# Both ways from the mixers to the experts, token tile by token tile

## The reference, cut to what matters

```python
def hier_moe(x, w_group, b_group, w_expert, b_expert, w1, w3, w2):       # second stage, 32 experts
    g_logits = xf @ w_group + b_group;  g_sel = argmax(g_logits);  g_w = softmax(g_logits)[g_sel]
    e_logits = (xf @ w_expert + b_expert)[the 8 of the group g_sel]
    e_top, e_loc = top_k(e_logits, 2);  gate = g_w * softmax(e_top)
    out[token] += gate * ((silu(x @ w1[e]) * (x @ w3[e])) @ w2[e])      # for its two experts

def expert_choice_ffn(h, w_router, w_gate, w_up, w_down):                # first stage, 16 experts
    aff = softmax(h @ w_router);  gate, idx = top_k(aff.T, 32)           # each expert takes 32 tokens
    y = (silu(h[idx] @ w_gate) * (h[idx] @ w_up)) @ w_down * gate        # added back at idx

def first_block(...):
    x = x + m2 * (mix @ w_out);  h = rmsnorm(x, norm2_g) * (1 + m4) + m3
    x = x + m5 * expert_choice_ffn(h, ...);  return rmsnorm(x, final_norm_g)
def second_block(...):
    h = h + g1 * ((ga * y_a + gb * y_b) @ w_out);  u2 = rmsnorm(h, norm2_g) * (1 + sc2) + sh2
    h = h + g2 * hier_moe(u2, ...);  return rmsnorm(h, final_g)
```

## Time and profile before

| what | value |
|---|---|
| median of three runs | 2306.96 us (2306.05 to 2314.09) |
| the profiled execution | 2308.12 us, its span 2306.3 us |
| TensorE matmul | 1898.4 us busy, 82% of the span |
| VectorE, ScalarE, GpSimd | 509.6, 319.9 and 97.7 us busy |
| moved by DMA | 728.67 MB, mean 316 GB/s |
| mean granted TensorE clock | 0.848 of full speed |

### The profile page before, as it was taken

How to read it: one execution, slowest core, us unless ns; L and a number is a source line. 1 busy time by engine, 2 the same in 40 slices (tenths; PEclk the granted TensorE clock), 3 DMA queues, 4 the chain that set the end, 5 groups by cost and what they waited for, 6 DMA issues and landing times.

```text
span 2306.3 us, 30312 instructions
## 1 busy us (share of the span) xinstructions
PE 1898.4 (82%) x12166; PEld 1059.0 (46%) x12166; DVE 509.6 (22%) x1047; ACT 319.9 (14%) x592; POOL 97.7 (4%) x125
## 2 busy tenths in 40 slices
PE   6999998867676767676766767799999599999997
PEld 3676776742222222222222222688788344444443
DVE  3224563330000000000000000342521312222222
ACT  3123331010000000000000000211520100000001
POOL 1012211000000000000000000000200000000000
PEclk9999999867667677777677676799999799999999
DMA  8214556079999999999999999244344699999997
GB/s 337 90 38 165 206 200 229 34 288 423 422 422 422 422 422 422 422 422 422 423 422 422 422 422 422 100 135 144 122 144 148 262 418 421 422 422 422 422 422 295
DMA packets 102752, 728.67 MB, mean 316 GB/s; under 512 B 11440, under 2 KB 12048, under 8 KB 16144
## 3 DMA queue, kind: packets, MB, share of 16 engines
q1 hardware_dynamic: 99504, 717.04, 76.4%
q10 hardware_dynamic: 3168, 10.49, 1.3%
HBM read 726.39 MB, written 1.10 MB: 315 GB/s over the span
## 4 chain that ended last, share of the span: by engine, by line
PE 66%; DMA 24%; DVE 4%; issue 3%; ACT 2%; POOL 0%; DVEq 0%; SPq 0%; ACTq 0%; POOLq 0%
DMA ring<-in_w_down 18%; PE psum L499 9%; PE psum L712 9%; PE psum L851 7%; PE psum L487 5%; PE psum L746 4%; DMA ring<-in_w_mod 4%; PE psum L1147 3%; PE psum L526 3%; PE psum L723 2%; PE psum L693 2%; DMA ring<-in_moe_w 2%; PE psum L1136 2%; PE psum L1081 2%; PE psum L979 2%
## 5 line engine op out<-in xcount | busy, mean ns | idle before, releaser
L499 PE MATMUL psum<-ring,main 128*32 128x512 f32 x2048 | 277.7, 692 | 85.0 <-ACT main L573 35.0
L518 PE MATMUL psum<-ring,main 128*32 128x512 f32 x1024 | 176.1, 808 | 84.8 <-DMA ring<-in_w_down 72.4
L712 PE MATMUL psum<-ring,main 128*64 128x512 f32 x1024 | 226.4, 594 | 2.3 <-DMA ring<-in_moe_w 1.3
L499 PEld LDWEIGHTS psum<-ring,main 128*32 128x32 f32 x2048 | 65.2, 123 | 281.0 <-issue 184.5
L851 PE MATMUL psum<-main,ring 128*128 128x256 f32 x768 | 169.2, 380 | 0.0
L851 PEld LDWEIGHTS psum<-main,ring 128*128 128x128 f32 x768 | 146.0, 190 | 21.7 <-issue 0.5
L712 PEld LDWEIGHTS psum<-ring,main 128*64 128x64 f32 x1024 | 72.5, 137 | 151.1 <-issue 149.8
L487 PE MATMUL psum<-main 128*128 128x32 f32 x512 | 112.5, 402 | 33.8 <-DVE main L551 33.8
L487 PEld LDWEIGHTS psum<-main 128*128 128x128 f32 x512 | 110.4, 332 | 57.5 <-DVE main L551 57.5
L518 PEld LDWEIGHTS psum<-ring,main 128*32 128x32 f32 x1024 | 30.7, 134 | 211.0 <-DMA ring<-in_w_down 145.1
L558 DVE TENSOR_TENSOR main<-main,psum 128x512 f32<-128x512 f32 x16 | 11.0, 688 | 525.1 <-ACT main L576 525.1
(11 more groups left out here) (422 smaller groups left out, 2056.5 us busy)
## 6 DMA issues: line engine op xcount, KB each, us to landing
ring<-in_moe_w SPq DMA_DIRECT2D x192, 1024.0 KB, 17.0
ring<-in_w_gate SPq DMA_DIRECT2D x128, 1024.0 KB, 25.9
ring<-in_w_up SPq DMA_DIRECT2D x128, 1024.0 KB, 25.9
ring<-in_w_down SPq DMA_DIRECT2D x128, 1024.0 KB, 20.4
ring<-in_w_mod SPq DMA_DIRECT2D x48, 1024.0 KB, 6.9
ring<-in_w_in SPq DMA_DIRECT2D x36, 1024.0 KB, 4.9
ring<-in_w_out SPq DMA_DIRECT2D x8, 1024.0 KB, 5.7
ring<-in_w_rnn_out SPq DMA_DIRECT2D x8, 640.0 KB, 3.9
```

Source lines behind the costliest of these rows:

```text
L499: last = mm(psum[32 * j:32 * j + 32, b, :], xg1[:, k, :], slot(n % SLOTS)[:, 512 * j:512 * j + 512], start=k == 0, stop=k == KT - 1)
L518: last = mm(psum[q:q + 32, BANK_Y, :], hidT[:, P * (f % 4) + 32 * (f // 4):P * (f % 4) + 32 * (f // 4) + 32], w[:, r, 512 * g:512 * g + 51 ...
L712: last = nc.tensor.matmul(psum[CAP2 * u:CAP2 * u + CAP2, b, :], xg2[:, 4 * h + k, CAP2 * u:CAP2 * u + CAP2], w[u][:, k, :], start=h == 0 a ...
```

## The change

- **First way.** The gain row is made before the late adds. The norm works on halves of a tile and signals each. The router holds the router weights as stationary operand, padded to 32 columns, four feature chunks side by side in the four column groups; the four partial sums are copied out and added by one matmul with a constant (`sum_experts`). It runs tile by tile, as do maximum, exponent, reciprocal and product. The rounds of the choice read PSUM in the first round instead of a copy; the product of the gates comes after the signal for positions; `slot` counts from 1, so the subtraction of 1 goes.
- **First expert stage.** One-hots of both tiles come first and have their own signal; gated ones follow (`m_gated`). ScalarE's two copies signal separately (`m_spread_sb`). A Silu of one column is called ahead of the loop.
- **Second way.** The projection goes tile by tile; norm, turn and router of tile 0 stand between the column blocks of tile 1. The norm takes two operations per half. The router holds 64 columns of weights, two chunks side by side. Three small operations of the choice are merged into others, the index and one-hots of a tile follow its choice at once, the gates of tile 1, the gated columns, the count and the flag come after the first one-hots. Only the three banks that the first gather uses are waited for ahead of it.
- **Loads.** SP loads slots 4 to 11 first, at `mixers_done`, then 0 to 3. In block 2 it loads six slots once the mixers' values are ready (`mix2_ready`), the other six behind the projection.

```diff
+    pe.wait_ge(m_gated, e + 1)
+    pe.wait_ge(m_spread_sb, e + 1)
...
-        pos = pg_tm[:, 0, t, bass.ds(e, 1)]
-        V.tensor_scalar(onehot[:, t, 0:CAP1], K("slot")[:, 0:CAP1], pos, None, ALU.is_equal)
+        last = V.tensor_scalar(onehot[:, t, 0:CAP1], K("slot")[:, 0:CAP1], pg_tm[:, 0, t, bass.ds(e, 1)], None, ALU.is_equal)
+    last.then_inc(m_onehot, 1)
+    for t in range(NT):
         last = V.tensor_scalar(gated[:, t, :].rearrange("p (g s) -> p g s", g=4),
                                K("slot")[:, 0:CAP1].unsqueeze(1).to_broadcast([P, 4, CAP1]),
-                               pos, pg_tm[:, 1, t, bass.ds(e, 1)], ALU.is_equal, ALU.mult)
-    last.then_inc(m_onehot, 1)
+                               pg_tm[:, 0, t, bass.ds(e, 1)], pg_tm[:, 1, t, bass.ds(e, 1)], ALU.is_equal, ALU.mult)
+    last.then_inc(m_gated, 1)
...
+    act.activation(xg1.rearrange("p k s -> p (k s)"), psum[:, BANK_X, 0:KT * CAP1], ACT.Copy).then_inc(m_xg, 1)
     act.wait_ge(m_spread, 2 * e + 1)
-    act.activation(xg1.rearrange("p k s -> p (k s)"), psum[:, BANK_X, 0:KT * CAP1], ACT.Copy)
-    act.activation(spread, psum[:, BANK_P, 0:S], ACT.Copy).then_inc(m_xg, 1)
+    act.activation(spread, psum[:, BANK_P, 0:S], ACT.Copy).then_inc(m_spread_sb, 1)
...
+    def project_out2(t, c):
+        key = ("wo2", t, c // 2)
         pe.wait_ge(*arrived(("w_out_2", c)))
         w = chunk(("w_out_2", c)).rearrange("p (k n) -> p k n", k=KT)
-        o = banks.new(("wo2", c))
-        pe.wait_ge(*banks.free(("wo2", c)))
...
+        if c % 2 == 0:
+            banks.new(key)
+            pe.wait_ge(*banks.free(key))
+        o = banks.tile(key)[:, 256 * (c % 2):256 * (c % 2) + 256]
         for k in range(KT):
-            last = mm(o[:, NE * t:NE * t + NE], u2T[:, k, P * t:P * t + P], w_rt2[:, k, :], start=k == 0, stop=k == KT - 1)
-    last.then_inc(banks.when_full("rt2"), 1)
+            last = mm(o, mixT2[:, k, P * t:P * t + P], w[:, k, :], start=k == 0, stop=k == KT - 1)
+        if c % 2:
+            last.then_inc(banks.when_full(key), 1)
+        last_user[("w_out_2", c)] = key
+
+    def turn_u2(t):
+        for g in range(2):
+            o = banks.new(("u2T", t, g))
+            pe.wait_ge(*banks.free(("u2T", t, g)))
+            pe.wait_ge(u2_ready, 2 * t + g + 1)
+            for c in range(4):
+                last = flip(o[:, P * c:P * c + P], u2[:, t, P * (4 * g + c):P * (4 * g + c) + P])
+            last.then_inc(banks.when_full(("u2T", t, g)), 1)
+
+    def route2(t):
+        o = banks.new(("rt2_part", t))
+        pe.wait_ge(*banks.free(("rt2_part", t)))
+        pe.wait_ge(wrt_loaded, 32)
+        for k2 in range(4):
+            if k2 % 2 == 0:
+                pe.wait_ge(*banks.read_out(("u2T", t, k2 // 2)))
+            for j in range(2):
+                last = mm(o[64 * j:64 * j + 64, 0:P], w_rt2[:, 2 * k2 + j, :], u2T[:, 2 * k2 + j, P * t:P * t + P], start=k2 == 0, stop=k2 == 3)
+        last.then_inc(banks.when_full(("rt2_part", t)), 1)
+
+    def route2_sum(t):
+        o = banks.new(("rt2", t))
+        pe.wait_ge(*banks.free(("rt2", t)))
+        pe.wait_ge(*banks.read_out(("rt2_part", t)))
+        mm(o[:, 0:NG2 + E2], rt2_part[:, t, :], K2("sum_experts_2"), start=True, stop=True).then_inc(banks.when_full(("rt2", t)), 1)
+
+    for c in range(4):
+        project_out2(0, c)
+    project_out2(1, 0)
+    project_out2(1, 1)
+    turn_u2(0)
+    project_out2(1, 2)
+    route2(0)
+    project_out2(1, 3)
+    route2_sum(0)
+    turn_u2(1)
+    route2(1)
+    route2_sum(1)
 
     o = banks.new("pos2")
     pe.wait_ge(*banks.free("pos2"))
     pe.wait_ge(masks_ready, 1)
     mm(o[:, 0:E2], K("tri_f"), masks[:, 0, :], start=True, stop=True)
     mm(o[:, E2:2 * E2], ones, masks[:, 0, :], start=True, stop=False)
-    mm(o[:, E2:2 * E2], K("tri_f"), masks[:, 1, :], start=False, stop=True)
-    mm(o[:, 2 * E2:3 * E2], ones, masks[:, 0, :], start=True, stop=False)
...
     for free in (n_gathered, n_gates, n_turned, n_spread):
         pe.sem_inc(free, 1)
-    gather2(pe, 0)
+    pe.wait_ge(masks_ready, 2)
+    mm(o[:, E2:2 * E2], K("tri_f"), masks[:, 1, :], start=False, stop=True).then_inc(banks.when_full("pos2"), 1)
+    o = banks.new("count2")
+    pe.wait_ge(*banks.free("count2"))
+    mm(o[:, 0:E2], ones, masks[:, 0, :], start=True, stop=False)
+    mm(o[:, 0:E2], ones, masks[:, 1, :], start=False, stop=True).then_inc(banks.when_full("count2"), 1)
+    used_first = (BANK_XG, BANK_XG + 1, BANK_P2)
+    assert banks.order["count2"] % 8 not in used_first, banks.order["count2"] % 8
+    for b in used_first:
+        pe.wait_ge(*banks.last(b))
+    gather2(pe, 0, first=True)
...
+    def route(t):
+        o = banks.new(("rt_part", t))
+        pe.wait_ge(*banks.free(("rt_part", t)))
+        pe.wait_ge(wrt_loaded, 16)
+        for k2 in range(2):
+            pe.wait_ge(*banks.read_out(("h2T", t, k2)))
+            for j in range(4):
+                last = mm(o[32 * j:32 * j + 32, 0:P], w_rt[:, 4 * k2 + j, :], h2T[:, 4 * k2 + j, P * t:P * t + P], start=k2 == 0, stop=k2 == 1)
+        last.then_inc(banks.when_full(("rt_part", t)), 1)
+        o = banks.new(("rt", t))
+        pe.wait_ge(*banks.free(("rt", t)))
+        pe.wait_ge(*banks.read_out(("rt_part", t)))
+        mm(o[:, 0:E1], rt_part[:, t, :], K("sum_experts"), start=True, stop=True).then_inc(banks.when_full(("rt", t)), 1)
...
-    for n in range(SLOTS):
-        if n == FRONT:
-            sp.wait_ge(mixers_done, 1)
-        if n < FRONT:
-            sp.wait_ge(*banks.full(last_user[holder1[n]]))
+    sp.wait_ge(mixers_done, 1)
+    for n in range(FRONT, SLOTS):
+        moe1_load(sp, 0, n)
+    for n in range(FRONT):
+        sp.wait_ge(*banks.full(last_user[holder1[n]]))
         moe1_load(sp, 0, n)
...
-    for n in range(12):
-        if n == FRONT:
-            sp.wait_ge(mixers_done, 2)
-        if n < FRONT:
-            sp.wait_ge(*banks.full(last_user[holder2[n]]))
+    sp.wait_ge(mix2_ready, KT // 2)
+    for n in (4, 5, 8, 9, 10, 11):
+        moe2_load(sp, 0, n)
+    for n in (0, 1, 2, 3, 6, 7):
+        sp.wait_ge(*banks.full(last_user[holder2[n]] if n < FRONT else ("wo2", 1, 1)))
...
+    act.activation(rstat[:, 31:32], half, ACT.Silu).then_inc(act_step, 1)
...
     for half_ in range(2):
         add_mix(1, half_, EARLY)
+    dve.wait_ge(rows_loaded[0], 64)
+    dve.wait_ge(gain_loaded, 16)
+    V.scalar_tensor_tensor(rows[:, 1, :], rows[:, 1, :], 1.0, gain, ALU.add, ALU.mult).then_inc(dve_step, 1)
+    dve.wait_ge(dve_step, dve_steps())
     for t in range(NT):
...
+    o = banks.tile("affT")[0:E1, 0:S]
+    for r in range(CAP1 // 8):
+        left = work if r else o
+        V.max(top8[0:E1, :], left).then_inc(dve_step, 1)
+        dve.wait_ge(dve_step, dve_steps())
+        V.match_replace(work, top8[0:E1, :], left, -1.0).then_inc(dve_step, 1)
+        dve.wait_ge(dve_step, dve_steps())
+    V.tensor_scalar(tmp, work, -1.0, None, ALU.is_equal).then_inc(dve_step, 1)
+    dve.wait_ge(dve_step, dve_steps())
+    V.tensor_tensor_scan(pos, a0, tmp, 0.0, ALU.mult, ALU.add).then_inc(dve_step, 1)
+    dve.wait_ge(dve_step, dve_steps())
+    V.tensor_tensor(pos, pos, tmp, ALU.mult).then_inc(dve_step, 1)
+    dve.wait_ge(dve_step, dve_steps())
+    dve.sem_inc(choice_ready, 1)
+    V.tensor_tensor(gat, o, tmp, ALU.mult).then_inc(banks.when_read("affT"), 1)
...
+    for half_ in range(2):
+        add_mix2(0, half_)
     dve.sem_inc(x3_ready, 1)
-    dve.sem_inc(mixers_done, 1)
     dve.wait_ge(rows_loaded[1], 48)
     dve.wait_ge(gain_loaded, 48)
     V.scalar_tensor_tensor(rows2[:, 1, :], rows2[:, 1, :], 1.0, acc2[:, 0, :], ALU.add, ALU.mult).then_inc(dve_step, 1)
     dve.wait_ge(dve_step, dve_steps())
-    dve.wait_ge(rstd_ready, 7)
-    for t in range(NT):
...
+    norm2_2(0)
+    for half_ in range(2):
+        add_mix2(1, half_)
+    dve.sem_inc(x3_ready, 1)
+    norm2_2(1)
...
+    gates_of(0)
     dve.wait_ge(*banks.full("pos2"))
-    o = banks.tile("pos2")
-    V.tensor_tensor(pos2, o[:, 0:2 * E2].rearrange("p (t e) -> p t e", t=NT), masks, ALU.mult).then_inc(dve_step, 1)
...
+    V.tensor_tensor(pos2, banks.tile("pos2")[:, 0:2 * E2].rearrange("p (t e) -> p t e", t=NT), masks, ALU.mult).then_inc(banks.when_read("pos2"), 1)
+    dve.wait_ge(*banks.read_out("pos2"))
+    dve.wait_ge(n_gathered, 1)
+    for t in range(NT):
+        for u in range(2):
+            last = V.tensor_scalar(onehot2[:, t, CAP2 * u:CAP2 * u + CAP2], K("slot"), pos2[:, t, u:u + 1], None, ALU.is_equal)
+    last.then_inc(n_onehot, 1)
+    gates_of(1)
+    for t in range(NT):
+        for u in range(2):
+            last = V.tensor_scalar(gated2[:, t, CAP2 * u:CAP2 * u + CAP2], K("slot"), pos2[:, t, u:u + 1], gates2[:, t, u:u + 1],
+                                   ALU.is_equal, ALU.mult)
+    last.then_inc(n_gated_first, 1)
```

(51 more changed lines are left out.)

253 lines of the change are left out of this document (105 added, 148 removed).

## The result

The changed kernel takes **2295.6 us** (median of 11 runs, 2284.1 to 2302.9), the kernel before 2308.6 beside it (11 runs, 2301.1 to 2314.1): ratio **0.9938, 95% interval 0.992 to 0.9956**. The profiled execution took 2295.71 us with a span of 2293.9, so 12.4 us less span than before.

The account below looks back on a forecast made before the run. Both expert stages were taken as bound by their weight stream (the second partly by TensorE), counted from their first up matmuls. 2308.12 - 7.7 (first way) - 16.3 (second way) = 2284.1 profiled, so median 2283; range 2276 to 2294.

Parts of the forecast that it names:

- The rule of the sum: Both expert stages: a microsecond earlier at either first up matmul is one less at the end, if twelve loads are in.
- I take 7.9: landing 463.7: First way: gain row lands 7.9 us after issue beside eight loads, at 463.7; last late add ends at 470.8.
- The late bound: First way: rows land only with all eight loads, at 478; late adds end at 485, up matmul 6.5 us later.
- Rows starve: Rival, first way: ScalarE's queue gets little while SP's is full, landing 478, time 2297 us; chance 0.06.
- One of the two ways is given back: Rival: product waits to about 470, or tables stay and second start finds 1.2 GHz; 2288 to 2293 us; chance 0.12.
- A + 27.95: First way: up matmul starts 27.9 to 28.0 us after the last late add ends, at 498.8, 7.7 us earlier.
- The gain product's new place: First way: product before the late adds, its 1.23 us falling into VectorE's idle 4.49 us before 461.26.
- that lower case: First way, rows in time: tile 1's adds wait only for TensorE, late adds end at 467.9, up 10.6 us earlier.
- The table load: First expert loop: the 1.28 us load before ScalarE's 0.39 us copy should go, a Silu being called before the loop.
- Second way: Second projection to second up matmul: up at 1816.4 instead of 1832.69, 16.3 us earlier, through router, choice and masks to gather.
- Clock: TensorE's rise from 1.2 GHz may shift: first gather up to 3 us shorter, second up to 2.5 shorter or 1 longer.
- clock rises sooner: Rival: rows land in time and the clock rises sooner in the first way, 2277 to 2280 us; chance 0.18.

Follow-up runs that it names:

- small_packets: Changed kernel with the first eight loads of the first experts each issued as two DMAs of 4 KB per partition: 2285.6 us, one run.
- rows_alone: Changed kernel, but SP issues its first loads of slots 4 to 11 only once norm rows and gain have landed: 2283.5 us, ratio 0.9869; again 2282.9, 0.9881.
- no_silu: Changed kernel without the Silu called ahead of the first expert loop: 2302.3 us, one run.
- rows_first_plus: rows_alone with the gain product back between the tiles' late adds and the gathered rows' copy released by the gather alone: 2284.7 us, ratio 0.9904.
- late_loads2: Changed kernel, but the second way's six early loads wait for the end of the projection: 2296.7 us, ratio 0.994.

## Why the prediction was wrong, point by point

- **The rule of the sum** holds: pairs keep their 29.0 and 29.8 us, and the span after the second up matmul is 473.6 us before (2306.3 - 1832.69) and 473.7 after (2293.9 - 1820.22).
- **"I take 7.9: landing 463.7"** is the step that failed. The gain landed at 473.0 (456.79 + 16.2). The end of the late adds, A, was to be at R + 17.05 (470.8 - 453.75) and came at R + 25.59 (480.31 - 454.72): **8.5 us**.
- **The late bound has the right kind of mechanism and a number that is near by luck.** With all eight loads first (landing 478, time 2297) it is the rival "Rows starve", and the result lies 1.4 us from its price. But the gain landed at 473.0, when 4.4 of the 8.4 MB had passed, and the first way lost 2.2 us and not the 6.5 of that bound; what it lacks cancels part of that: the kernel before stood at 2308.6 and not 2307, and the start and the stage between took 1.5 us more. The rival "One of the two ways is given back" (0.12) names the very wait, to about 470, and prices it at 2288 to 2293; the wait ended 3 us later. I gave "Rows starve" 0.06 and excluded it with the Trainium skill's rule ("DMA: Bandwidth & Descriptors", Queues, rings and completion order) that an engine alternates between queues packet by packet. The trace agrees that the queues alternate: 638 packets against 602. It doesn't agree with the packet of 9 to 17 descriptors that the Trainium skill gives there, if a record of the trace is a descriptor: the turns here are single records (small_packets). And the rule doesn't protect a queue whose packets are small; read in bytes it speaks against this change.
- **A + 27.95** was 29.39 (509.70 - 480.31). 1.07 of the 1.44 us lie before the turned affinities (A + 13.02 for 11.95). Most of that is the router of tile 0: with its copy and sum it ended at A + 6.96 (486.69 + 0.58) where the forecast has A + 6.05, and TensorE turns tile 1 only behind it, so the last turned half was copied out at A + 9.38 (489.09 + 0.60) and not 8.65. The rest lies in the router passes of tile 1 and their sum. 0.46 lie from there to the gather (7.76 for 7.3); from gather to up 8.61 for 8.65.
- **The gain product's new place** was to cost when the row is late, which is right. With the rows undisturbed it earns nothing: A is at R + 15.01 in rows_alone (469.25) and was at R + 15.09 before. I had put that lower case at R + 14.15, by TensorE; VectorE's chain from the landing row ends it, four half tiles of 1.45 and the product.
- **The table load** left the path as forecast, for another reason (no_silu): the split of ScalarE's waits hides it, and the Silu ahead of the loop only takes 32 hidden loads out. The rule I weighed against, that loads are placed per block ("ScalarE activation tables: per-element evaluation and per-set limits", Table sets in the compiler and the runtime), gave 1.3 us less for the first way. The trace doesn't agree with it as I read it: the same loop, unchanged inside, has no load with the Silu ahead of it and 32 without.
- **Second way: 16.3 forecast, 16.1 measured**, and term by term: router read 8.0 (7.9 forecast), choice 4.7 (4.6), masks to gather 3.3 (3.8), and 0.2 from gather to up that was not forecast. Reading: 1807.04, 1810.40 and 1813.30 less 1765.97, against 1811.39, 1819.41 and 1825.61 less 1762.31. The projection lost 2.2 us (30.06 for 27.89) to the turns and the router in it; the forecast writes 2.95 where its own two terms, 2.0 and 1.3, add up to 3.3.
- **Clock**: in the bounds given; 0.50 during the first gather (500 to 505 us), 1.00 as the second stage starts (1820 to 1825). The rival "clock rises sooner" did not come in the first way:

```profile
500.00:505.00 5.00, 3.91 (x19) 3.91 (x19) 0.90 (x4) 0.00 (x0) 0.00 (x0) 0.50 0.00 0
1820.00:1825.00 5.00, 4.78 (x23) 1.99 (x25) 0.59 (x3) 0.03 (x1) 0.00 (x0) 1.00 0.00 0
```

The forecast for the profiled execution was 2284.1; it took 2295.7. Of the 11.6 us, 8.5 are the rows' landing, 1.4 the chain behind A, 1.0 the start that came later before the change begins, 0.5 the stage between, and 0.2 the second way. With the landing repaired (rows_alone) the kernel takes 2283.5 and 2282.9, the number forecast, but that match is partly luck: the kernel before took 2312.2 and 2310.5 beside it and not 2307, so it gained 28.7 and 27.6 us where 24 were forecast. Its first way is 8.7 us shorter (52.79 - 44.07) where 7.7 were forecast.

## What to carry to other kernels

Before a load is moved up beside small transfers of another queue, count packets: the small ones wait for as many large packets as they have packets of their own, all those queued ahead of them on their queue included. Let what the next engine waits for land first, or issue it ahead on the same queue; here two waits on SP are worth 10.9 us of the chain, and the early loads that they delay had earned nothing. And an operation that waits for a transfer doesn't belong in front of work that is ready, least of all when the same change makes that transfer later.

## What the runs showed of the hardware

- Two DMA queues took turns packet for packet: 638 and 602 packets in 19 us, 694 and 681 in 15 us with the loads' packets halved, while the shares of bytes went from 30:70 to 44:56.
- The delay goes by what the load queue moves while the rows are under way, not by what is issued there. With none ahead of the rows, and the product waiting for them, it starts at R + 7.9 to 8.3. Two loads (2.1 MB) put it at R + 13.8, halved packets (2.5 MB moved) at R + 14.3, and eight loads (4.4 MB moved of 8.4) at R + 18.4 to 18.9: 5.9, 6.4 and 10.6 us later, 2.4 to 2.8 us for each MB.
- A table load of 1.28 us can move 16 us ahead of its activation or stand right before it, with only the waits in front of the activation changed (496.82 before 512.96; 504.45 before 505.7).
- TensorE's granted clock was at 0.50 (1.2 GHz) soon after the late projection began, behind an idle stretch of 3.1 to 3.5 us, and rose to 1.00 (2.4 GHz) at different times in different kernels: the same 32 passes took 10.16 us in the changed kernel, 8.86 in the kernel before and in rows_first_plus, 9.36 in rows_alone and 8.69 in late_loads2. The last has the same early loads as the changed kernel, so they don't decide it. The stretch from 460 to 462 us in the changed kernel, whose projection began at 458.74 and whose clock was still 0.50 from 463 to 464, and in rows_first_plus, whose projection began at 457.13 (length, busy times, then the clock, DMA share and GB/s):

```profile
460.00:462.00 2.00, 2.00 (x6) 1.55 (x6) 0.00 (x0) 0.00 (x0) 0.00 (x0) 0.50 0.99 406
```

```profile
460.00:462.00 2.00, 2.00 (x9) 1.66 (x9) 1.11 (x2) 0.00 (x0) 0.00 (x0) 0.81 0.23 84
```

It cost the changed kernel nothing, because the gain row was later still. Why the rise came later is open.
